# Prompt attention: transposes moved two steps behind the scores over a third row of weights, and query stacks built on GpSimd

## What is computed

```python
s_c = q . kc * scale + bias          # 63 compressed blocks
s_s = q . k_selected * scale + bias  # all blocks up to the own one (16 of 16 blocks are selected)
s_w = q . k_window * scale + bias    # a window of 512 tokens: up to 5 blocks of 128
o = g[0] * softmax(s_c) . vc + g[1] * softmax(s_s) . v_sel + g[2] * softmax(s_w) . vw
```

## Time and profile before

| | us |
|---|---|
| median of 3 runs | 2248.26 (2247.31 to 2249.77) |
| the profiled execution | 2254.18 |
| its span | 2252.4 |
| attention: first to last matmul | 582.35 to 876.6 |
| first work of the next stage | 878.4 |

### The profile page before, as it was taken

One profiled execution on the slowest core, in us unless ns is written; L12 is line 12 of the kernel. 1 busy time (PEld: TensorE's weight loads), 2 busy tenths in 40 slices (PEclk: granted clock), 3 DMA queues, 4 the chain that ended last, 5 costly groups with the idle time before them and its releaser, 6 DMA issues. The chain is left out here.

```text
span 2252.4 us, 33438 instructions
## 1 busy us (share of the span) xinstructions
PE 2067.2 (92%) x13773; PEld 1957.6 (87%) x13773; DVE 761.2 (34%) x1447; ACT 503.5 (22%) x918; POOL 613.1 (27%) x505
## 2 busy tenths in 40 slices
PE   6999989995588888999999799999999999997897
PEld 4999989964476777999989799999999999997786
DVE  2202623332766766112241433203312222234412
ACT  3111011131466566001011321110000000011323
POOL 1322400000344445333333113233323323221110
PEclk6999999986799999999999899999999999998898
DMA  5323263224300000111113121121111111113011
GB/s 147 125 84 123 42 234 150 75 77 187 110 2 1 1 2 25 43 54 42 46 43 113 38 104 47 35 58 43 42 45 50 46 41 53 47 35 127 24 47 78
DMA packets 164799, 151.08 MB, mean 67 GB/s; under 512 B 24747, under 2 KB 157389, under 8 KB 161934
## 3 DMA queue, kind: packets, MB, share of 16 engines
q1 hardware_dynamic: 160846, 111.68, 16.3%
q0 software_dynamic: 2304, 33.56, 3.8%
q10 hardware_dynamic: 1536, 4.23, 0.5%
HBM read 132.54 MB, written 21.10 MB: 68 GB/s over the span
## 5 line engine op out<-in xcount | busy, mean ns | idle before, releaser
L580 PE MATMUL ffn_acc<-HH,WS 128*128 128x344 f32 x2112 | 394.9, 321 | 9.0 <-DVE HL L512 7.8
L588 POOL CAST WS<-W 128x1024 fp32r<-128x1024 f32 (+2 forms) x125 | 130.7, 1046 | 901.1 <-PE ffn_acc L580 539.6
L580 PEld LDWEIGHTS ffn_acc<-HH,WS 128*128 128x128 f32 x2112 | 344.3, 189 | 9.4 <-issue 7.8
L590 POOL TENSOR_TENSOR WS<-W,WS 128x1024 fp32r<-128x1024 f32 (+2 forms) x125 | 294.9, 2360 | 10.0
L580 PE MATMUL ffn_acc<-HL,WS 128*128 128x344 f32 x1056 | 224.8, 321 | 0.0
L580 PE MATMUL ffn_acc<-AH,WS 128*128 128x344 f32 x1056 | 195.4, 320 | 0.0
L580 PE MATMUL proj_acc<-HH,WS 128*128 128x344 f32 x912 | 174.3, 323 | 6.3 <-DVE HL L512 6.3
L580 PEld LDWEIGHTS ffn_acc<-HL,WS 128*128 128x128 f32 x1056 | 179.4, 190 | 0.0
L1852 POOL TENSOR_SCALAR Hr<-Hr,tiny,gtok 128x63 f32<-128x63 f32 (+4 forms) x192 | 125.1, 661 | 174.1 <-DVE tiny L1932 141.3
L580 PEld LDWEIGHTS ffn_acc<-AH,WS 128*128 128x128 f32 x1056 | 171.6, 188 | 0.0
L580 PEld LDWEIGHTS proj_acc<-HH,WS 128*128 128x128 f32 x912 | 148.9, 189 | 8.3 <-issue 5.8
(11 more groups left out here) (388 smaller groups left out, 3280.7 us busy)
## 6 DMA issues: line engine op xcount, KB each, us to landing
W<-in_w_in SPq DMA_DIRECT2D x30, 512.0 KB, 3.8
W<-in_w_ffn_gate SPq DMA_DIRECT2D x22, 512.0 KB, 3.8
W<-in_w_ffn_up SPq DMA_DIRECT2D x22, 512.0 KB, 3.9
X<-kept_x SPq DMA_DIRECT2D x2, 4128.0 KB, 13.1
W<-in_w_ffn_down SPq DMA_DIRECT2D x16, 384.0 KB, 3.4
W<-in_w_ffn_down SPq DMA_DIRECT2D x16, 320.0 KB, 3.0
kept_x<-Z SPq DMA_DIRECT2D x1, 4128.0 KB, 15.8
Z<-kept_x SPq DMA_DIRECT2D x1, 4128.0 KB, 13.7
```

The lines of the kernel that those rows point to most:

```text
L580: last = k.nc.tensor.matmul(acc[:, s, n, 0:NW], k.WS[:, ws, part, c, :], src[:, c, n * NW:(n + 1) * NW], start=(c == 0 and part == 0 and s ...
L588: k.nc.gpsimd.tensor_copy(k.WS[:, ws, 0, 0:nk, :], w).then_inc(hi_done, 1)
L590: k.nc.gpsimd.tensor_tensor(k.WS[:, ws, 1, 0:nk, :], w, k.WS[:, ws, 0, 0:nk, :].bitcast(F32), ALU.subtract).then_inc(split_done, 1)
```

## The change

The transposes of a step run two steps after its scores, between selected and window scores; the products of a pair follow two pairs back. `PR` has a third row, and a fourth place for transposed weights, both in X's part of SBUF, so X comes back in three pieces, two of them when the last users of that part are done. The row sums `l` have a third place. ScalarE copies transposed groups of s - 2 before the exponentials of s. `queries` moves from VectorE to GpSimd: the queries are negated in place first, then copied and subtracted. It runs twice at the start and then after the scaling of every fourth step.

```diff
-        PR = [k.Hr[:, 0:1792], k.Hr[:, 1792:3584]]
-        flat = [k.Hr[:, 3584:5376], k.Hr[:, 5376:7168]]
...
+        xr = k.X[:].rearrange("p c t -> p (c t)")
+        PR = [k.Hr[:, 0:1792], k.Hr[:, 1792:3584], xr[:, 5920:7712]]
+        flat = [xr[:, 4128:5920], k.Hr[:, 3584:5376], k.Hr[:, 5376:7168]]
...
-        l = [small[:, 6:9], small[:, 9:12]]
+        l = [small[:, 6:9], small[:, 9:12], small[:, 12:15]]
...
         def turned(s, j):
-            if s % 3 < 2:
-                return flat[s % 3][:, j * P:(j + 1) * P]
+            if s % 4 < 3:
+                return flat[s % 4][:, j * P:(j + 1) * P]
...
         @block.sync
         def _(sp):
-            sp.dma_start(k.X[:].rearrange("p c t -> p (c t)"), k.kept).then_inc(x_back, 16)
+            sp.dma_start(xr[:, 0:4 * N], k.kept[:, 0:4 * N]).then_inc(x_back, 16)
             sp.dma_start(k.kvtok[:, 0:8, 256:384], weight(k.g["w_in"], GB0)).then_inc(k.first_in, 16)
             sp.dma_start(k.kvtok[:, 0:4, 512:640], weight(k.g["w_branch_gm"], 0)).then_inc(k.first_in, 16)
             sp.wait_ge(k.first_in, 32)
-            sp.wait_ge(x_back, 16)
+            sp.wait_ge(pv_done, S // 2 - 1)
+            sp.dma_start(xr[:, 4 * N:5 * N], k.kept[:, 4 * N:5 * N]).then_inc(x_back, 16)
+            sp.wait_ge(pt_done, g0[S - 1])
+            sp.dma_start(xr[:, 5 * N:8 * N], k.kept[:, 5 * N:8 * N]).then_inc(x_back, 16)
+            sp.wait_ge(x_back, 48)
...
-                        last = nc.tensor.transpose(tp[:, g % 3, j * P:(j + 1) * P], PR[s % 2][:, a:a + P], k.ident[:])
+                        last = nc.tensor.transpose(tp[:, g % 3, j * P:(j + 1) * P], PR[s % 3][:, a:a + P], k.ident[:])
...
-            pe.wait_ge(cleared, 3)
-            for s in range(S):
-                selected_scores(s)
-                window_scores(s)
-                if s % 2 == 0 and s >= 4:
-                    products(s // 2 - 2, 1)
-                if s % 2 == 1 and s >= 3:
-                    products(s // 2 - 1, 0)
-                if s:
-                    turns(s - 1)
-            products(S // 2 - 2, 1)
-            turns(S - 1)
-            products(S // 2 - 1, 0)
-            products(S // 2 - 1, 1)
+            pe.wait_ge(cleared, 4)
+            for s in range(S + 4):
+                if s < S:
+                    selected_scores(s)
+                if 2 <= s < S + 2:
+                    turns(s - 2)
+                if s < S:
+                    window_scores(s)
+                if s >= 4:
+                    products(s // 2 - 2, s % 2)
...
         @block.scalar
         def _(act):
             def selected_exps(s):
                 t, c, gr, wb = plan[s]
-                if s >= 2:
-                    act.wait_ge(pt_done, g0[s - 1])
-                pr, b, w = PR[s % 2], s % 2, (t + 1) * P
+                if s >= 3:
+                    act.wait_ge(pt_done, g0[s - 2])
+                pr, b, w = PR[s % 3], s % 2, (t + 1) * P
...
-            def copies(s, groups):
-                for q in groups:
...
+            def copies(s):
+                for q in range(ng[s]):
                     if copier[g0[s] + q][0] == "act":
                         act.wait_ge(pt_done, g0[s] + q + 1)
-                        if s >= 3:
-                            act.wait_ge(pv_done, (s - 3) // 2 + 1)
+                        if s >= 4:
+                            act.wait_ge(pv_done, s // 2 - 1)
                         dst, src = evacuate(s, q)
                         nc.scalar.activation(dst, src, ACT.Copy).then_inc(act_copied, 1)
...
-            act.wait_ge(cleared, 2)
-            for s in range(S):
-                early = ng[s - 1] // 2 if s else 0
-                selected_exps(s)
-                if s % 2 == 0 and s >= 4:
-                    output(s // 2 - 2)
-                if s:
-                    copies(s - 1, range(early))
-                window_exps(s)
-                if s:
-                    copies(s - 1, range(early, ng[s - 1]))
-            output(S // 2 - 2)
-            copies(S - 1, range(ng[S - 1]))
-            output(S // 2 - 1)
+            act.wait_ge(cleared, 3)
+            for s in range(S + 5):
+                if s % 2 == 0 and s >= 6:
+                    output((s - 6) // 2)
+                if 2 <= s < S + 2:
+                    copies(s - 2)
+                if s < S:
+                    selected_exps(s)
+                    window_exps(s)
...
         @block.gpsimd
         def _(pool):
+            def queries(i):
+                t, c = plan[4 * i][0:2]
+                q = k.Q[:, c, 0:T].rearrange("p (t n) -> p t n", n=P)[:, t:TT - t:TT - 1 - 2 * t, :]
+                if i >= 2:
+                    pool.wait_ge(scored_w, 4 * (i - 1))
+                nc.gpsimd.tensor_scalar(q, q, -1.0, None, ALU.mult).then_inc(q_minus, 1)
+                pool.wait_ge(q_minus, i + 1)
+                for gr in range(2):
+                    own = slice(gr * HD, (gr + 1) * HD)
+                    nc.gpsimd.tensor_copy(QT[own, i % 2, :, gr, :], q[own]).then_inc(q_hi, 1)
+                for gr in range(2):
+                    own, other = slice(gr * HD, (gr + 1) * HD), slice((1 - gr) * HD, (2 - gr) * HD)
+                    pool.wait_ge(q_hi, 2 * i + 2)
+                    nc.gpsimd.tensor_tensor(QT[other, i % 2, :, gr, :], q[own], QT[own, i % 2, :, gr, :].bitcast(F32),
+                                            ALU.subtract).then_inc(q_ready, 1)
+                    pool.wait_ge(q_ready, 4 * i + 2 * gr + 1)
+                    nc.gpsimd.tensor_copy(k.QZ[own, i % 2, :, gr, :], QT[own, i % 2, :, gr, :].bitcast(F32)).then_inc(q_ready, 1)
+                    pool.wait_ge(q_ready, 4 * i + 2 * gr + 2)
+            pool.wait_ge(cleared, 4)
+            queries(0)
+            queries(1)
             for s in range(S):
                 t, c, gr, wb = plan[s]
                 h = c + 4 * gr
                 for j, (a, w, ready) in enumerate(((0, (t + 1) * P, factor_s), (1024, len(wb) * P, factor_w), (1664, NCP, factor_w))):
                     r = (j + 1) % 3
-                    x = PR[s % 2][:, a:a + w]
+                    x = PR[s % 3][:, a:a + w]
                     pool.wait_ge(ready, s + 1)
                     nc.gpsimd.tensor_scalar(x, x, li[s % 2][:, j:j + 1], k.gtok[:, t, 3 * h + r:3 * h + r + 1], ALU.mult, ALU.mult).then_inc(p_ready, 1)
+                if s % 4 == 3 and s // 4 + 2 < S // 4:
+                    queries(s // 4 + 2)
...
         @block.vector
         def _(dve):
-            def queries(i):
...
-                for gr in range(2):
-                    own = slice(gr * HD, (gr + 1) * HD)
-                    nc.vector.tensor_scalar(QT[own, i % 2, :, gr, :], q[own], -1.0, None, ALU.mult).then_inc(q_hi, 1)
-                for gr in range(2):
-                    own, other = slice(gr * HD, (gr + 1) * HD), slice((1 - gr) * HD, (2 - gr) * HD)
-                    dve.wait_ge(q_hi, 2 * i + gr + 1)
-                    nc.vector.scalar_tensor_tensor(out=QT[other, i % 2, :, gr, :], in0=q[own], scalar=-1.0,
-                                                   in1=QT[own, i % 2, :, gr, :].bitcast(F32), op0=ALU.mult,
-                                                   op1=ALU.subtract).then_inc(q_ready, 1)
-                    nc.vector.tensor_copy(k.QZ[own, i % 2, :, gr, :], QT[own, i % 2, :, gr, :].bitcast(F32)).then_inc(q_ready, 1)
...
-            for b in range(2):
+            for b in range(3):
                 nc.vector.memset(PR[b][:, 1664:1792], 0.0).then_inc(cleared, 1)
...
-            dve.wait_ge(cleared, 3)
-            queries(0)
-            queries(1)
-            for s in range(S):
-                selected_minima(s)
-                if s:
+            dve.wait_ge(cleared, 4)
+            for s in range(S + 2):
+                if s < S:
+                    selected_minima(s)
+                if 1 <= s < S + 1:
                     window_inverses(s - 1)
-                window_minima(s)
-                selected_inverse(s)
-                if s:
-                    copies(s - 1)
-                if s % 4 == 3 and s // 4 + 2 < S // 4:
-                    queries(s // 4 + 2)
-            window_inverses(S - 1)
-            copies(S - 1)
+                if s < S:
+                    window_minima(s)
+                    selected_inverse(s)
+                if s >= 2:
+                    copies(s - 2)
```

More of the change, by code:

```diff
@@ L1638, in prompt_attention @@
         op = st.psum("op", [P, 512])
-        q_hi, q_ready, scored_s, scored_w, biased, neg_s, neg_w, exp_s, exp_w, factor_s, factor_w, p_ready, pt_done, act_copied, dve_copied, pv_done, o_copied, cleared, x_back = st.sems(
-            "q_hi q_ready scored_s scored_w biased neg_s neg_w exp_s exp_w factor_s factor_w p_ready pt_done act_copied dve_copied pv_done o_copied cleared x_back")
-        PR = [k.Hr[:, 0:1792], k.Hr[:, 1792:3584]]
-        flat = [k.Hr[:, 3584:5376], k.Hr[:, 5376:7168]]
```

(39 more changed lines are left out.)

8 lines of the change are left out of this document (2 added, 6 removed).

## The result

| | before | after |
|---|---|---|
| median of 4 runs, us | 2249.02 (2247.31 to 2250.64) | 2222.33 (2214.35 to 2231.01) |
| the profiled execution, its span | 2254.18, 2252.4 | 2231.01, 2228.9 |
| attention, first to last matmul | 582.35 to 876.9: 294.6 | 585.56 to 843.38: 257.8 |
| TensorE busy, idle in it | 248.0, 46.5 | 238.0, 19.9 |
| last matmul to first work of the next stage | 1.5 | 5.9 |

A forecast was written before the change was run, and what follows sets the result against it. TensorE bounds prompt attention, busy for 247.7 of 294.2 us. Its idle time falling from 46.5 to 19 us (-27.5), start +2.1 and end +4.7 make -20.7: a median of 2227.6 us, range 2213 to 2250.

The forecast's parts named there:

- the window at the start: TensorE's idle time in the first window of attention: from 5.2 us to 2.5.
- waits behind the stacks: In the attention loop, transposes wait for GpSimd scalings delayed by query stacks: 9 us new over fourteen calls.
- the small waits: Places without slack in the attention cycles, mainly around the window scores: 0.4 us a cycle, 6.4 us in 16 cycles.
- drain: TensorE's idle time at the end of attention: 1 us, where the old one idles 0.8.
- Part 1: Transposes two steps late: TensorE's work unchanged, GpSimd wait gone, window scores' wait covered by transposes, 6.4 us left.
- Part 2: Query stacks on GpSimd: 4.15 us a call, 9 us of new wait; relieving VectorE worth nothing by itself.
- signs of being wrong: Query calls over 5.6 us, window scores waiting over 15 us, or ScalarE idling on a transpose group while minima are ready.
- Parts 3 and 4: Ends of attention: first scores 2.1 us later; stage closes 4.7 us later, X coming back in three pieces.
- A: Rival: query stacks on GpSimd don't show, slack in the attention cycle covers them; 2218.6 us, chance 0.15.
- B: Rival: the window scores' chain stays half exposed, 13.5 us in some 45 waits; 2241 us, chance 0.18.
- C: Rival: GpSimd becomes the bound; at 5.6 us a call the gain is gone, at 8 us 2281 us; chance 0.12.
- D: Rival: VectorE's 128x1 minima wait for GpSimd instructions reading SBUF, 14 us in 32 waits; 2242 us, chance 0.05.

The follow-up runs named there:

- e3: Changed kernel with transposes still two steps late but back behind the products, ScalarE's copies back around the window exponentials: 2240.91 us, ratio to before 0.9966.
- e4: Changed kernel with GpSimd's query stacks one step later, behind the scaling of the next cycle's first step: 2208.55 us, ratio to before 0.9809.
- e7: Changed kernel with whole query stacks on VectorE, between reciprocals and window minima in each cycle's first step: 2220.44 us, ratio to before 0.9882.
- e1: Changed kernel with the query stacks back on VectorE at their old place, behind the copies of every fourth step: 2216.76 us, ratio to before 0.9863.
- e5: Changed kernel with X's late pieces cut at their last users, 1168 and 896 KB: 2220.82 us, ratio to before 0.9879.
- e9: Changed kernel with query stacks on VectorE in two halves, in each cycle's first two steps, and X's late pieces cut at last users: 2210.85 us, ratio 0.9821.

## Why the prediction was right, point by point

**Total and idle time.** Forecast: idle time from 46.5 to 19 us, median 2227.6. Measured: 19.9 us, 2222.33. By parts, forecast then measured: the window at the start 2.5, 3.7; waits behind the stacks 9, 12.4 in 14 (12.8 with the start); the small waits 6.4, 3.1 (15.5 us of idle time in the loop less 12.4); drain 1, 0.7. Two errors of 3 us cancelled. In the median there is more luck: the stage with its ends gained 30 us where the forecast had 20.7. The median came only 5.3 us under the forecast because the rest of the program, and a median of the kernel before that was 0.8 us higher with its fourth run, took back 4 of those 9.

**Part 1, the size of "TensorE's busy time unchanged" was wrong.** It fell from 248.0 to 238.0 us with the same 2288 matmuls, and that is why the stage gained 36.7 us where the sum had 27.5. In the loop, at one clock, it fell by 8.1 (214.9 to 206.9). The page counts the drain of the last matmul as busy, and I had used "some 0.2 us" of it per wait in Part 2, but not in the sum. The runs order themselves so: 214.9 and 215.8 with both kinds of waits, 211.3 with the window's alone, 208.2 to 205.2 with few or none. TensorE's waits in the loop number 53 before, 36 in e3, 23 after and 13 in e4, so the busy time falls by some 0.24 us a wait (9.6 us for 40). No run changes the number of waits alone, and e7, with 29 waits and 207.1 us, lies 2 us under that line: that it is the drains, is argued and not shown. The rest, 2 us, is the start: 19.0 us busy in the first window at a clock of 0.72 before, 15.3 at 0.81 after, of which 1.7 moved to the drain; as that clock differed between runs of like kernels, I don't put it down to the change.

**Part 1, the reason for the window wait was the wrong one.** I wrote that the wait "gets the transposes as cover". But between two window scores TensorE did the same work before (products, transposes, selected scores: 3.2 us), and still waited. What shrank is the chain: 713.42 to 717.46 was 4.0 us before, not the 2.85 that I added up; I had left out the 1.3 us between minima and exponentials, in which ScalarE stood at its copies. e3 has the lag without the new place, and has that 1.3 us and 25.9 us of window waits. The forecast held since 2.85 is the chain of the new order: window scores end at 687.07, the last read at 689.76, the next window scores start at 689.84, just covered, as I had it. Of GpSimd's wait the reason was right: e3 shows none. One of the signs of being wrong did come, too: nine times in the loop ScalarE idled on L0's late transposes while H0's selected minima were ready, for 0.07 to 0.15 us, and three times, at t = 2, for 0.5 (2.3 us in all; at 733.31 the copy began, the minima were ready at 732.77). Nearly no wait of the window scores came of it.

**Part 2, the stacks.** 4.39 us from call to call (581.12 to 585.51) where I had 4.15. By shape:

```profile
L1856 POOL TENSOR_TENSOR QT<-Z,QT 64x256 fp32r<-64x256 f32 x32 | 23.2, 726 | 2.7
...
L1848 POOL TENSOR_SCALAR Z<-Z 128x256 f32<-128x256 f32 x16 | 13.6, 851 | 6.3 <-DVE QZ L1950 6.2
L1852 POOL CAST QT<-Z 64x256 fp32r<-64x256 f32 x32 | 12.6, 394 | 2.0
L1859 POOL CAST QZ<-QT 64x256 fp32r<-64x256 f32 x32 | 12.6, 392 | 2.1
```

Casts (0.40) and subtractions (0.73) came out as worked from the two widths, shifted partitions included. The scaling took 0.85 in place of 0.56: the row of the same width has another operand form. That makes the missing 0.24 us a call. 14 x 0.24 is 3.4 us, just what the waits came out longer, but it does not lie where it should: they were 1.2 to 1.4 us at t = 0 (forecast 1.1), 0.8 to 0.9 at 1 (0.75), 1.1 to 1.2 and once 0.7 at 2 (0.65), and 0.25 to 0.5 at 3 (none). At 2 and 3, which have 2.6 of the 3.4 us, the cover was also taken too large. "Worth nothing by itself" of VectorE's relief holds at the old place (e1), since there the stacks delay a scaling from either engine; that the place itself was the cost, 13.5 us, I did not ask.

**Parts 3 and 4.** Start +2.3 (forecast 2.1), end +4.4 (4.7): the pieces of 516 and 1548 KB landed in 3.9 and 7.2 us, 8.2 forecast for the second. e5 shows 2.9 of it to be the cut.

**Rivals.** A (stacks don't show) is refuted by the 12.4 us; its number, 2218.6, is closer to the median than the forecast's (3.7 us off, beside 5.3), but by the fallen busy time. B by 0.8 us of window waits. C: 4.39 us a call is under the 5.6 of break-even. D: the minimum of line 1920 took 153, 155 and 401 ns (least, median, most), no more than the earlier trace rows, while GpSimd was busy for 73% of the loop, in place of 43% (less than the twice of the prediction).

**Figures that don't follow from their rows.** The 0.4 us a cycle of Part 1 is a seventh and not a fifth of the idle time (2.75 us in the mean of the four kinds of cycle). Without hand-over Part 2's terms give 3.6 us, not 3.4. A call of 4.8 us adds 14 x 0.65 = 9 us by rival C's own rule, not 6, which puts the upper end of the range at 2253. The result depends on none of them.

## What to carry to other kernels

Between two steps of a software pipeline, ask of each in-order queue what stands between a result and its user: here the window wait was made by a copy queued ahead of the exponentials, whose transposes came late, and GpSimd's by a stack queued ahead of a scaling. Moving work to an idle engine gave nothing until it stood behind the instruction that the bound engine asks for next: at the old place either engine gave the same, and on GpSimd the place was worth 13.5 us. On VectorE the new place paid only with the work cut in halves. Take idle time away and the busy time in the profile can fall too, here by 8.1 us in the loop; and a buffer borrowed from a later load should be given back in pieces cut at its last users.

## What was not expected of the hardware

VectorE's small fp32 operations between SBUF operands and GpSimd's stretch one another. In e1, whose GpSimd idles beside them, the operation with two inputs took 420 ns in the mean and the cast 288; in e7 the first took 597 in the mean (0.82 us for the one at 689.91), in e9 they took 550 and 516, while GpSimd's 128x640 scaling went from 876 ns (after) to 970. In e9:

```profile
L1849 POOL TENSOR_SCALAR Hr<-Hr,tiny,gtok 128x640 f32<-128x640 f32 x26 | 25.2, 970 | 21.8 <-DVE tiny L1929 17.1 <-DVE tiny L1923 4.7
...
L1865 DVE SCALAR_TENSOR_TENSOR QT<-Z,QT 64x256 fp32r<-64x256 f32 x32 | 17.6, 550 | 1.1
L1868 DVE CAST QZ<-QT 64x256 fp32r<-64x256 f32 x32 | 16.5, 516 | 1.0
```

In e1 the 64x256 scalings that began with GpSimd's 128x896 lasted up to 1.09 us (the median of all 32 is 0.29), which is what a 128x896 scaling takes undisturbed (1.09). The Trainium skill, page "SBUF — State Buffer", section "Who interferes with whom", says so of VectorE's copies, casts and scalings in their two-port modes and of its two-input operations: one engine holds the shared ports for a whole instruction, the other blocks. These traces agree, in sizes of 0.1 to 0.8 us; for the 128x1 minimum they show at most 0.25 us in some of 32.
